# Pairing the value products of two attentions, sharing the stationary tile of two heads' keys, and one product of halves for the highest frequencies

## The reference, cut to what matters

```python
# windowed attention, 8 query heads, 2 key heads (in the profile: gqa)
s = einsum('bnqhgd,bnkhd->bnhgqk', q, kw) * scale - slopes * dist   # band of 3 x 128 keys
probs = e / (sum(e) + exp(sink - m));  o = einsum('bnhgqk,bnkhd->bnqhgd', probs, vw)

# latent attention, 8 heads (in the profile: mla)
kv = (rms_norm(c_kv, kv_norm) @ w_ukv).reshape(B, S, 8, 64 + 64)    # 128 rows of weights
k_nope, v = kv[..., :64], kv[..., 64:]
s = (einsum(q_nope, k_nope) + einsum(q_rope, k_r)) * scale
o = einsum('bhqk,bkhd->bqhd', softmax(s), v)

# Fourier mixing: transform over 512 tokens and over 256 channels in each of 4 groups, real part
f = jnp.fft.fftn(hg, axes=(1, 3), norm='ortho').real                # then o_b @ w_branch_b
```

## Time and profile before

| | |
|---|---|
| median of 3 runs | 2994.45 us (2993.39 to 2995.41) |
| the profiled execution: time, span of the core | 2992.27 us, 2990.5 us |
| PE busy | 2936.1 us, 98% |
| PE weight loads busy (beside the matmuls) | 2395.4 us, 80% |
| DVE, ACT, POOL busy | 1221.1 (41%), 1290.7 (43%), 1457.5 us (49%) |
| loaded and stored | 269.49 MB and 2.10 MB, 91 GB/s |
| granted TensorE clock, mean | 0.995 of 2.4 GHz |

### The profile page before, as it was taken

One profiled execution on the slowest core, in us unless ns is written; L12 is line 12 of the kernel. 1 busy time (PEld: TensorE's weight loads), 2 busy tenths in 40 slices (PEclk: granted clock), 3 DMA queues, 4 the chain that ended last, 5 costly groups with the idle time before them and its releaser, 6 DMA issues.

```text
span 2990.5 us, 40057 instructions
## 1 busy us (share of the span) xinstructions
PE 2936.1 (98%) x14304; PEld 2395.4 (80%) x14304; DVE 1221.1 (41%) x2077; ACT 1290.7 (43%) x2009; POOL 1457.5 (49%) x826
## 2 busy tenths in 40 slices
PE   8999999999989999999999989999999999999999
PEld 7877887888878777887888878768888887788887
DVE  5546444221053555434222070564555128455510
ACT  4556545222243556444223263654444237444421
POOL 4665455444445755555444454544444444444443
PEclk9999999999999999999999999999999999999999
DMA  4222242333322232333333322203333333233333
GB/s 142 72 85 71 78 127 85 98 98 99 106 85 85 71 92 59 94 116 104 96 94 105 106 76 93 64 4 103 98 98 93 97 99 92 85 98 94 96 109 88
DMA packets 77240, 273.27 MB, mean 91 GB/s; under 512 B 8760, under 2 KB 9400, under 8 KB 77120
## 3 DMA queue, kind: packets, MB, share of 16 engines
q1 hardware_dynamic: 74112, 266.05, 28.9%
q10 hardware_dynamic: 3008, 5.57, 0.5%
HBM read 269.49 MB, written 2.10 MB: 91 GB/s over the span
## 4 chain that ended last, share of the span: by engine, by line
PE 92%; DVE 4%; ACT 2%; issue 1%; POOL 1%; DMA 0%; SPq 0%; DVEq 0%; ACTq 0%; POOLq 0%
PE ps L726 25%; PE ps L728 25%; PE ps L727 25%; PE ps L1005 2%; PE ps L1030 2%; PE ps L1221 2%; PE ps L1227 1%; PE ps L1222 1%; PE ps L987 1%; PE ps L1112 1%; PE ps L1118 1%; PE ps L1113 1%; PE ps L982 1%; POOL WLO L2648 1%; PE ps L798 0%
## 5 line engine op out<-in xcount | busy, mean ns | idle before, releaser
L2648 POOL TENSOR_TENSOR WLO<-WRAW,WHI 128x1024 fp32r<-128x1024 f32 x467 | 1125.8, 2414 | 1244.6 <-ACT WHI L1389 1244.6
L726 PE MATMUL ps<-HH,WHI 128*128 128x512 f32 x2184 | 858.2, 393 | 1.2 <-POOL WLO L2648 0.9
L728 PE MATMUL ps<-HH,WLO 128*128 128x512 f32 x2184 | 851.6, 390 | 0.0
L727 PE MATMUL ps<-HL,WHI 128*128 128x512 f32 x2184 | 850.9, 390 | 0.0
L1389 ACT ACTIVATE WHI<-WRAW 128x1024 fp32r<-128x1024 f32 x467 | 490.7, 1052 | 333.1 <-DMA WRAW<-wall 332.5
L726 PEld LDWEIGHTS ps<-HH,WHI 128*128 128x128 f32 x2184 | 410.3, 188 | 89.0 <-issue 4.8
L728 PEld LDWEIGHTS ps<-HH,WLO 128*128 128x128 f32 x2184 | 410.2, 188 | 86.1
L727 PEld LDWEIGHTS ps<-HL,WHI 128*128 128x128 f32 x2184 | 410.6, 188 | 83.1
L2505 DVE SCALAR_TENSOR_TENSOR ps<-U,COLS,ps 128x512 f32<-128x512 f32 x192 | 145.1, 756 | 121.0 <-ACT ps L1837 106.9
L2056 DVE TENSOR_TENSOR ACC<-ACC,SQ 128x512 f32<-128x512 f32 x80 | 70.5, 881 | 286.0 <-ACT SQ L1673 271.2
L728 PE MATMUL ps<-F2H,WLO 128*128 128x512 f32 x384 | 149.5, 389 | 0.0
(11 more groups left out here) (393 smaller groups left out, 4688.8 us busy)
## 6 DMA issues: line engine op xcount, KB each, us to landing
WRAW<-wall SPq DMA_DIRECT2D x502, 512.0 KB, 3.5
y<-X ACTq DMA_DIRECT2D x8, 256.0 KB, 3.9
X<-xin SPq DMA_DIRECT2D x3, 512.0 KB, 8.3
DFT<-dft ACTq DMA_DIRECT2D x4, 258.0 KB, 4.1
PT_IN<-pin ACTq DMA_DIRECT2D x2, 512.0 KB, 3.6
DIL<-dil ACTq DMA_DIRECT2D x1, 768.0 KB, 4.2
X<-xin SPq DMA_DIRECT2D x2, 256.0 KB, 5.0
COLS<-cols ACTq DMA_DIRECT2D x1, 290.5 KB, 6.0
```

The lines of the kernel that those rows point to most:

```text
L726: pe.matmul(out_, WHI[w_at], x_hi, start=first, stop=False)
L727: pe.matmul(out_, WHI[w_at], x_lo, start=False, stop=False)
L728: return pe.matmul(out_, WLO[w_at], x_hi, start=False, stop=last)
L2648: pool.tensor_tensor(WLO[:, s, :], whole, WHI[:, s, :].bitcast(F32), ALU.subtract).then_inc(wt_lo, 1)
```

## The change

1. **Value products by pairs of items.** In both hosts the value products of items q-4 and q-3 are issued together in iterations with even q from 4 to 18, and none in those with odd q. Everything else keeps its place in the iteration.
2. **Keys of two heads in one stationary tile.** The unit of `w_ukv` is packed with the key columns of all heads first and the value columns behind. `mla_heads` makes 4 key tiles of 128 columns in place of 8 of 64, alternating with the 4 value tiles. DVE reads each key tile in two operations of 64 partitions (`key_pair`); the fourth pair is read in iteration 0 of `branch_mla`. ACT takes the first two splits of keys (`score_hi` 2 and 3) and the split of the next weights in between the value tiles. PE's wait for the last key tile at the start of the attention goes.
3. **Highest frequencies in one product of halves.** WN and NY become F32R. Rows 0 to 3, 32 to 35 and 64 to 67 of one 128-row product hold the high, low and high halves of NY against the high, high and low halves of WN, so one F32R matmul takes the place of the F32 one. The weights' rows are loaded three times into WNRAW; ACT copies WNRAW to WN, DVE writes the remainder of rows 64 to 67; ACT copies NY twice where it did once, and DVE writes its remainder.

```diff
@@ fourier_branch and branch_mla on PE
-                    if q > DEPTH:
-                        value_products(att, q - DEPTH - 1)
+                    if q > DEPTH and (q - DEPTH) % 2 == 0:
+                        for behind in (2, 1):
+                            value_products(att, q - DEPTH - behind)
@@ mla_heads on PE
-                for h in range(MLA_H):
+                vals = slice(MLA_H * MLA_NOPE, MLA_H * P)
+                for i in range(ST):
+                    k = key_tile(i)
                     pe.wait_ge(bank_free[st.bank(k)], st.use(k))
-                    three(ps[st.bank(k)][0:MLA_NOPE, :], (slice(None), s, slice(h * P, h * P + MLA_NOPE)),
-                          hi[:, QT, :], lo[:, QT, :], True, True).then_inc(S["part_multiplied"], 1)
+                    three(ps[st.bank(k)][:, :], (slice(None), s, slice(i * P, (i + 1) * P)), hi[:, QT, :], lo[:, QT, :],
+                          True, True).then_inc(S["part_multiplied"], 1)
+                    k = value_tile(i)
...
@@ attention_ready on PE
                 if st.mode == "mla":
                     pe.wait_ge(S["rope_keys_spread"], st.rope.at("rope_keys_spread", 1))
-                    pe.wait_ge(bank_free[st.qk.bank(2 * MLA_H - 1)], st.qk.use(2 * MLA_H - 1) + 1)
@@ fourier on ACT
-                act.dma_start(WN[0:FGROUPS, :], wnyq[st.l]).then_inc(S["nyquist_loaded"], 16)
+                for at in NYQUIST_ROWS:
+                    act.dma_start(WNRAW[at:at + FGROUPS, :], wnyq[st.l]).then_inc(S["nyquist_loaded"], 16)
...
+                act.wait_ge(S["nyquist_loaded"], st.at("nyquist_loaded", 48))
+                act.activation(WN[:, :], WNRAW[:, :], ACT.Copy).then_inc(S["nyquist_hi_ready"], 1)
...
+                for at in (0, 64):
+                    act.activation(by_frequency(NY[at:at + FGROUPS, :]), by_parity(ps[st.bank(k)][0:FGROUPS, 0:UH]), ACT.Copy)\
+                       .then_inc(S["nyquist_hi_ready"], 1)
@@ mla_heads on ACT
-                act.wait_ge(unit_used, st.unit(4))
-                split_of(st, 4)
-                for n in range(2, 4):
-                    score_hi(st.att, n)
                 for t in range(ST):
-                    k = 2 * 4 + MLA_H + t
+                    if t == 1:
+                        score_hi(st.att, 2)
+                        score_hi(st.att, 3)
+                    if t == 2:
+                        split_of(st, 4)
+                    k = value_tile(t)
@@ fourier on DVE, after the folds of tokens
+                at = slice(64, 64 + FGROUPS)
+                dve.wait_ge(S["nyquist_hi_ready"], st.at("nyquist_hi_ready", 1))
+                dve.tensor_tensor(WN[at, :], WNRAW[at, :], WN[at, :].bitcast(F32), ALU.subtract).then_inc(S["nyquist_lo_ready"], 1)
...
+                k, at = NYQUIST, slice(32, 32 + FGROUPS)
+                dve.wait_ge(S["nyquist_hi_ready"], st.at("nyquist_hi_ready", 3))
+                dve.tensor_tensor(by_frequency(NY[at, :]), by_parity(ps[st.bank(k)][0:FGROUPS, 0:UH]), by_frequency(NY[0:FGROUPS, :].bitcast(F32)), ALU.subtract)\
+                   .then_inc(bank_free[st.bank(k)], 1)
@@ mla_heads and branch_mla on DVE
-                for h in range(MLA_H):
-                    k = MLA_H + h
-                    dve.wait_ge(S["part_multiplied"], st.at("part_multiplied", 4 + h + 1))
-                    scaled(st, k, 0, KA[0:MLA_NOPE, h, :], ps[st.bank(k)][0:MLA_NOPE, :], RBK[0:MLA_NOPE, :])
+                key_pair(st, 0)
+                key_pair(st, 1)
                 for n in range(2, 4):
                     score_lo(st.att, n)
+                key_pair(st, 2)
...
+            def key_pair(st, i):
+
+                k = key_tile(i)
+                dve.wait_ge(S["part_multiplied"], st.at("part_multiplied", 4 + 2 * i + 1))
+                dve.tensor_tensor(KA[0:MLA_NOPE, 2 * i, :], ps[st.bank(k)][0:MLA_NOPE, :], RBK[0:MLA_NOPE, :], ALU.mult)
+                scaled(st, k, 0, KA[0:MLA_NOPE, 2 * i + 1, :], ps[st.bank(k)][MLA_NOPE:P, :], RBK[MLA_NOPE:P, :])
```

More of the change, by code:

```diff
@@ L315, in plan @@
         pr.op_hi = op_hi
-        f = add("fourier", tiles=2 * ST + 2 * FGROUPS + 1, per={"channels_transformed": 8, "tokens_transformed": 9, "operand_hi_ready": 8, "dft_loaded": 32, "nyquist_cleared": 2, "nyquist_loaded": 16, "tokens_folded": 4}, op=op, made=start, l=l)
+        f = add("fourier", tiles=2 * ST + 2 * FGROUPS + 1, per={"channels_transformed": 8, "tokens_transformed": 9, "operand_hi_ready": 8, "dft_loaded": 32, "nyquist_cleared": 2, "nyquist_loaded": 48, "nyquist_hi_ready": 3, "nyquist_lo_ready": 1, "tokens_folded": 4}, op=op, made=start, l=l)
         cq = add("cq_norms", per={"cq_square_ready": QT + 1, "cq_square_added": QT - 1, "cq_summed": 1, "cq_mean_ready": 2, "cq_factors_ready": 1, "cq_spread": 2, "cq_rows_ready": 2}, proj=pr)
@@ L328, in plan @@
         rp = add("rope", tiles=1, per={"rope_rotated": 1, "cos_applied": 1, "rope_added": 1, "rope_keys_doubled": 1, "rope_keys_spread": 1}, proj=pr)
-        heads = add("mla_heads", units=5, tiles=20, per={"part_multiplied": 4 + 11, "rope_scaled": 1}, op=need_cq, made=cq)
+        heads = add("mla_heads", units=5, tiles=16, per={"part_multiplied": 4 + 7, "rope_scaled": 1}, op=need_cq, made=cq)
         bm = add("branch_mla", units=2 * (DT - 2), tiles=16, per={"gate_ready": DT - 2, "product_ready": DT - 2}, kt=GQA_H // 2, src="OC", op=need_oc, t=2)
@@ L464, in build @@
         OBH, OBL = work("OBH", [P, DT, UH], 53, F32R), work("OBL", [P, DT, UH], 61.5, F32R)
-        WF, WN, NY = work("WF", [P, FOLDED, 2 * FGROUPS * P], 70), work("WN", [P, DM], 78), work("NY", [P, UH], 82)
+        WF, WN, NY = work("WF", [P, FOLDED, 2 * FGROUPS * P], 70), work("WN", [P, DM], 78, F32R), work("NY", [P, UH], 82, F32R)
         MG = work("MG", [P, DT, SEQ], 84)
@@ L914, in mla_heads @@
                 pe.wait_ge(S["operand_ready"], st.op + QT + 1)
-                for h in range(MLA_H):
+                vals = slice(MLA_H * MLA_NOPE, MLA_H * P)
+                for i in range(ST):
+                    k = key_tile(i)
                     pe.wait_ge(bank_free[st.bank(k)], st.use(k))
-                    three(ps[st.bank(k)][0:MLA_NOPE, :], (slice(None), s, slice(h * P, h * P + MLA_NOPE)),
-                          hi[:, QT, :], lo[:, QT, :], True, True).then_inc(S["part_multiplied"], 1)
-                    k += 1
-                for t in range(ST):
+                    three(ps[st.bank(k)][:, :], (slice(None), s, slice(i * P, (i + 1) * P)), hi[:, QT, :], lo[:, QT, :],
+                          True, True).then_inc(S["part_multiplied"], 1)
+                    k = value_tile(i)
                     pe.wait_ge(bank_free[st.bank(k)], st.use(k))
[L922 to L929, removed]
+                    o, at = ps[st.bank(k)][:, :], slice(i * P, (i + 1) * P)
+                    pe.matmul(o, hi[:, QT, at], WHI[:, s, vals], start=True, stop=False)
+                    pe.matmul(o, lo[:, QT, at], WHI[:, s, vals], start=False, stop=False)
+                    pe.matmul(o, hi[:, QT, at], WLO[:, s, vals], start=False, stop=True).then_inc(S["part_multiplied"] if i < ST - 1 else unit_used, 1)
             def rope(st):
@@ L1591, in score_hi @@
                 if n == 6:
-                    act.wait_ge(bank_free[st.qk.bank(2 * MLA_H - 1)], st.qk.use(2 * MLA_H - 1) + 1)
+                    act.wait_ge(bank_free[st.qk.bank(key_tile(3))], st.qk.use(key_tile(3)) + 1)
                 act.wait_ge(bank_free[st.qk.bank(k)], st.qk.use(k) + 1)
@@ L2159, in branch_mla @@
                         scores_read(att, q)
+                    if q == 0:
+                        key_pair(att.qk, 3)
                     if 1 <= q <= att.heads * ST:
@@ L2653, in fourier @@
             def fourier(st):
-                pool.memset(WN[:, :], 0.0).then_inc(S["nyquist_cleared"], 1)
-                pool.memset(NY[:, :], 0.0).then_inc(S["nyquist_cleared"], 1)
+                pool.memset(WNRAW[:, :], 0.0).then_inc(S["nyquist_cleared"], 1)
+                pool.memset(NY[:, :].bitcast(F32), 0.0).then_inc(S["nyquist_cleared"], 1)
             def remainder_early(n):
```

17 lines of the change are left out of this document (12 added, 5 removed).

## The result

| | before | after |
|---|---|---|
| median of 4 runs on the same chip | 2994.47 us (2993.39 to 2995.41) | 2975.78 us (2974.73 to 2978.21) |
| ratio | | 0.9943 [0.9932, 0.9955] |
| the profiled execution: time, span | 2992.27 us, 2990.5 us | 2978.21 us, 2975.2 us |

The change saves 18.7 us, 0.62%. The forecast was 2976.2 us.

What follows compares the result with a forecast made beforehand. PE was taken to bound the kernel (92% of the chain), so PE's increments were summed: 7.8 (pairs) + 5.5 (keys) + 5.0 (highest frequencies) = 18.3 us saved, predicted median 2976.2 us, range 2972 to 2982.5.

Steps and rivals of the forecast that it cites:

- The line through groups of 8, 12 and 16 records: Value products on PE: each record adds 0.054 us, and each group pays 0.16 once on entry.
- Rival A: Ahead of mla's first scores: POOL's remainder holds DVE's second `score_lo`, scores start 2.2 us late, 4.4 less saved, 2980.6; chance 0.09.
- The covers that I took as nothing: Highest frequencies: idle time hides ACT's added copy (1.05 us a layer otherwise) and DVE's remainders (1 us at most).
- rival E: Slower: row loads land late, holding ACT's copy into WN, all eight OBH and PE; needs 11 us lateness; chance 0.02.
- caught up after three: Highest frequencies on DVE: the first OBL is 1.3 us late, recovered after three through 0.46 us idle ahead of each.
- Rival B: Short odd mla iterations wait for exponentials held by POOL remainders: 0.9 us in each of 6 a layer, 11 us, 2987; chance 0.06.
- The bounds 2972.5 and 2979: Forecast's own bounds in us: lower from gqa's upper bound and 1 us scatter, upper with part 3's covers gone, 2 x 1.05.

Runs made afterwards that it cites:

- e1: Changed kernel with value products item by item again in both attentions; keys and highest frequencies stay changed: 2984.32 us, 0.9971 of before.
- e2: Changed kernel with value products paired in mla only, gqa's item by item again: 2979.08 us, 0.9954 of before.
- e4: Changed kernel with the highest frequencies in one plain F32 product as before, without the added copies and remainders: 2979.14 us, 0.9956 of before.
- e3: Changed kernel with the keys of each head in a tile of its own, as before: 2980.58 us, 0.9956 of before.
- The doses: One or two extra DVE row maxima per mla item: 2992.45 and 2996.12 us on the kernel before, 2978.13 and 2982.53 on the changed kernel.
- b1: Changed kernel with one ACT weight split ahead of the sigmoid and mla's first split and remainder moved to iteration 1: 2974.55 us, 0.9936 of before.
- e5: Changed kernel with all value products of one head, then the other, instead of turns between partition halves: 2991.76 us (one execution).

## Why the prediction was right, point by point

```
us a layer                      forecast      measured on the chain
mla's pairs                     2.5           2.6, 2.5      (e1 - e2)
gqa's pairs                     1.4           1.5           (e1, e2 - after)
keys                            2.76          2.8           (rope to first scores)
highest frequencies             2.48          2.52          (e4 - after)
sum of both layers              18.3          18.7          (before - after)
```

**PE's increments as the unit of account.** Every term was read from steps of the chain, not from durations (0.39 us for a matmul that adds 0.23), and each came out within 0.1. The parts also add, 2 x (2.5 + 1.5 + 2.8 + 2.5) = 18.6, so little is lost or won between them. That the median came within 0.4 us of the forecast is closer than medians can tell here, 3.4 us to either side; the terms on the chain are the evidence.

**Part 1.** The line through groups of 8, 12 and 16 records held at 32, which took 1.90 (forecast 1.88), and the 0.88 of the odd turns was the 0.87 that behind scores stood already in the trace. For gqa I chose between 0.12 and 0.31 for a place that the trace did not show. The choice, 0.16 by the nearest change of array form, was right: e2's turn of 6 in 0.80 beside 0.81 after. e1 and e2 are 1.50 a layer behind the kernel after in gqa, where 7 x 0.16 + 0.31 = 1.43.

**Part 2.** The matmuls went, and almost nothing came in their place: in layer 0 the second scores start 4.37 behind the first where it was 4.20, in layer 1 4.22 as before. The cover was as thin as forecast: in the kernel after, on DVE and POOL,

```profile
238.72 1.29 DVE L2289 TENSOR_TENSOR KL<-KA,KH 128x512 fp32r<-128x512 f32 x2
```

```profile
228.29 10.42 POOL L2677 TENSOR_TENSOR WLO<-WRAW,WHI 128x1024 fp32r<-128x1024 f32 x4 [6.61 <-ACT WHI L1397]
240.40 2.40 POOL L2677 TENSOR_TENSOR WLO<-WRAW,WHI 128x1024 fp32r<-128x1024 f32 x1 [1.69 <-ACT WHI L1397]
```

the two `score_lo` stand at 238.72 to 240.01, behind POOL's four remainders (which end at 238.71) and ahead of the next (240.40). Rival A did not come, with 0.4 us to spare at the later end and none at the earlier, where DVE came to them as POOL ended (238.68 and 238.71). The forecast had just this place, 242.1 and 242.14 in the rows of before, so the fit was foreseen; that a margin of nothing held is luck, and e3 shows a case where it didn't. Rival A's price of 2.2 was also too high: PE waits for each head's `score_lo` by itself, so with the second one held the three matmuls of the first head (0.69) would have gone ahead, and 1.5 is left. The Trainium skill (SBUF — State Buffer, Who interferes with whom) calls this an exclusive lock for a DVE instruction with two SBUF inputs against a GpSimd one that reads SBUF. The rows of e3 and of before agree (0.67 free, 2.19 and 2.49 beside POOL). The other page that I weighed, the Trainium skill (TensorEngine Tiling (Array Packing), Key Properties), has the array drained at a change of tiling mode. By it, at the rows' 0.31, the keys would have brought 3.07 a layer; measured was 2.8. For F32R matmuls of 128 x 64 behind 128 x 128 the rows don't agree with it, for the value products and for gqa's scores they do. Whether the price belongs to the form or to plain F32 on two halves of the partitions no run here tells.

**Part 3.** The covers that I took as nothing were nothing. ACT's idle time ahead of the first OBH is 2.14 where it was 3.09, less by the copy of 1.05, which starts at 84.98 with its rows landed, so rival E had nothing to stand on. On DVE, in the kernel after:

```profile
88.71 1.22 DVE L2110 TENSOR_TENSOR WN<-WNRAW,WN 4x1024 fp32r<-4x1024 f32 x1
89.96 1.10 DVE L2114 TENSOR_TENSOR OBL<-ps,OBH 128x258 fp32r<-128x258 f32 x3
91.43 0.43 DVE L2114 TENSOR_TENSOR OBL<-ps,OBH 128x258 fp32r<-128x258 f32 x1 [0.38 <-ACT OBH L1495]
```

The remainder of 1.22 (forecast 1.3) makes the first OBL late, three follow without a pause, and at the fourth DVE waits for ACT again: "caught up after three".

**Rival B** stayed away, partly for the reason that I gave against it. In the kernel after NM takes 0.97 for item 1 (the wait of 0.6) and 1.06 for item 3; from item 4 on it is held four times (items 4, 6, 10 and 12: 1.93, 1.08, 1.09, 1.09), each time in an even iteration, which lasts 7.05 us. All later odd items take 0.17, item 7 by a hair: POOL's remainder ends at 281.18 and its NM starts at 281.27. So the remainder was over before the next NM, as forecast, but with 0.1 us to spare there. The doses put the price on it: 0.9 us of slack in an odd iteration, against up to 1.9 by which a remainder can hold NM. In b1 it happened once.

**What was off.** Only small things. The profiled execution took 2978.21 where I had 2974.0 for its like: 4.2 more, of which 1.2 lie outside the span (3.0 after, 1.8 before) and 3.4 in stages that the change doesn't touch (18.7 saved in the touched ones, 15.3 in the span), less 0.4 by which the sum was low. The bounds 2972.5 and 2979 don't follow from the terms named for them, which give 2976.2 - 2.1 - 1 = 2973.1 and, with the same 1 us of scatter, 2976.2 + 2.1 + 1 = 2979.3; the range does not hang on it. That DVE held the first scores of the kernel before by 0.1 us I had not seen, nor that a `score_lo` was already slowed there by POOL.

## What to carry to other kernels

When one engine fills the chain, count what each instruction adds there (differences of starts, or a line through groups of several sizes), and price an edit in these; four terms worked out so came within 0.1 us a layer. Going into a group of plain F32 matmuls with 64 output columns and out again cost PE 0.3 us here, while F32R matmuls with 64 columns of weights cost nothing of the kind, so look which changes have a price, sum up how often the order of work makes one, and let small products wait for each other as long as their buffers allow. Shortening an iteration takes slack from the engines beside it: measure it with a dose of added work before the next cut, since here 0.9 us is left, and moving one remainder by an iteration lost as much at a later wait as it gained at the first.

## What the runs showed of the hardware that was not expected

- F32 products of 64 output columns, with 128 columns of data, cost 0.055 us a record when the two halves of the output partitions take turns, and 0.083 one half after the other (e5, the slope between groups of 20 and 32 records; with turns the same two groups give 0.055). So the halves seem to overlap in part: the order has a cost, but one half alone does not take twice the time.
- Leaving such a group costs the next transposes 0.15 us, whichever order the halves had (1.02 in the kernel after and in e5), and leaving scores of 64 rows costs the same (0.81 for 6 transposes, 0.65 behind F32R matmuls).
- A DVE instruction on 128 x 2 elements, 0.17 us by itself, took up to 1.93 us beside one remainder on POOL in the mla attention of layer 0, as long as a large one is held, and the exponentials of both heads are behind it.
